# A chunked recurrence on TensorE: small products grouped by kind over six heads, and a state held in two buffers

## What is computed

```python
def second_block(x, ...):
    h = rmsnorm(x, pre_mix_g[l])
    ya, yb, yc = jnp.split(h @ w_in[l], [A_COLS, A_COLS + B_COLS], axis=-1)
    mix = jnp.concatenate([rwkv7_mixer(ya, ...), moba_mixer(*jnp.split(yb, 3, axis=-1)),
                           gmlp_mixer(...)], axis=-1) @ w_out[l]
    ...

def rwkv7_mixer(...):
    ...
    def step(state, inp):                       # once per token, 512 tokens
        r_t, w_t, k_t, v_t, kk_t, a_t = inp
        sa = jnp.einsum('bhij,bhj->bhi', state, -kk_t)
        state = (state * w_t[:, :, None, :]
                 + sa[..., :, None] * (kk_t * a_t)[:, :, None, :]
                 + v_t[..., :, None] * k_t[:, :, None, :])
        return state, jnp.einsum('bhij,bhj->bhi', state, r_t)
    _, y = lax.scan(step, s0, xs)
```

## Time and profile before

| | |
|---|---|
| median of three runs | 3281.07 us (3279.92 to 3281.27) |
| the profiled execution, first to last instruction (span) | 3270.9 us |
| its granted TensorE clock, mean | 0.987 |
| TensorE (PE) busy | 3179.8 us, 97% of the span |
| TensorE's weight loads (PEld) busy | 1976.4 us, 60% |
| VectorE (DVE) busy | 1372.5 us, 42% |
| ScalarE (ACT) busy | 598.2 us, 18% |

### The profile page before, as it was taken

How to read it: one execution, slowest core, us unless ns; L and a number is a source line. 1 busy time by engine, 2 the same in 40 slices (tenths; PEclk the granted TensorE clock), 3 DMA queues, 4 the chain that set the end, 5 groups by cost and what they waited for, 6 DMA issues and landing times.

```text
span 3270.9 us, 35828 instructions
## 1 busy us (share of the span) xinstructions
PE 3179.8 (97%) x14634; PEld 1976.4 (60%) x14634; DVE 1372.5 (42%) x2564; ACT 598.2 (18%) x1240; POOL 1.4 (0%) x6
## 2 busy tenths in 40 slices
PE   8999999999999999999999999999999999999998
PEld 5855554334333433458786588888546444688887
DVE  4256530111111111165743364466353894364655
ACT  2143220110010001121442320102332002120001
POOL 0000000000000000000000000000000000000000
PEclk9999999999999999999997999999999999999999
DMA  6122369999999999931000222222111222222221
GB/s 268 60 78 93 114 250 411 428 428 429 429 428 429 429 428 429 428 138 37 26 1 1 93 87 78 86 95 103 55 52 52 77 77 77 77 78 103 78 78 52
DMA packets 43100, 585.39 MB, mean 179 GB/s; under 512 B 4768, under 2 KB 6816, under 8 KB 7648
## 3 DMA queue, kind: packets, MB, share of 16 engines
q1 hardware_dynamic: 42752, 582.45, 43.8%
q0 software_dynamic: 224, 1.18, 0.1%
HBM read 581.51 MB, written 2.10 MB: 178 GB/s over the span
## 4 chain that ended last, share of the span: by engine, by line
PE 87%; DMA 9%; DVE 3%; ACT 1%; issue 1%; SPq 0%; DVEq 0%; ACTq 0%
PE PS L482 20%; PE PS L294 11%; PE PS L1670 11%; PE PS L686 10%; DMA ring<-in_weights 5%; PE PS L1648 4%; DMA A<-in_weights 4%; PE PS L1246 3%; PE PS L374 2%; PE PS L1593 2%; PE PS L348 2%; PE PS L1634 1%; PE PS L1575 1%; PE PS L2198 1%; PE PS L1038 1%; PE PS L1203 1%
## 5 line engine op out<-in xcount | busy, mean ns | idle before, releaser
L482 PE MATMUL PS<-A 128*128 128x256 f32 x1336 | 298.4, 380 | 0.0
L1670 PE MATMUL PS<-ring,A 128*64 128x512 f32 x1248 | 284.8, 599 | 1.5 <-DMA ring<-in_weights 0.6
L482 PEld LDWEIGHTS PS<-A 128*128 128x128 f32 x1336 | 254.1, 190 | 35.1 <-issue 0.8
L294 PE MATMUL PS<-H,ring 128*128 128x512 f32 x544 | 234.4, 593 | 0.7 <-issue 0.7
L1752 DVE TENSOR_TENSOR A<-A,PS 64x512 f32<-64x512 f32 x64 | 44.1, 690 | 434.6 <-ACT A L1699 434.6
L482 PE MATMUL PS<-H,ring 128*128 128x256 f32 x784 | 185.3, 380 | 0.8 <-ACT A L1785 0.8
L1670 PEld LDWEIGHTS PS<-ring,A 128*64 128x64 f32 x1248 | 82.7, 136 | 168.0 <-issue 160.8
L294 PEld LDWEIGHTS PS<-H,ring 128*128 128x128 f32 x544 | 103.5, 190 | 130.0 <-issue 130.0
L1670 PE MATMUL PS<-A 128*64 128x512 f32 x784 | 178.4, 598 | 2.0 <-DMA A<-in_weights 0.8
L686 PE MATMUL PS<-A 128*128 128x256 f32 x800 | 178.7, 379 | 0.0
L1648 PE MATMUL PS<-A 128*64 128x512 f32 x768 | 174.3, 598 | 3.4 <-DMA A<-in_weights 3.1
(11 more groups left out here) (534 smaller groups left out, 4126.9 us busy)
## 6 DMA issues: line engine op xcount, KB each, us to landing
ring<-in_weights SPq DMA_DIRECT2D x176, 2048.0 KB, 14.2
A<-in_weights SPq DMA_DIRECT2D x96, 2048.0 KB, 24.3
X<-in_x SPq DMA_DIRECT2D x1, 2048.0 KB, 12.9
H<-in_weights SPq DMA_DIRECT2D x1, 2048.0 KB, 13.6
A<-in_weights SPq DMA_DIRECT2D x2, 768.0 KB, 23.8
vec<-in_vec SPq DMA_DIRECT2D x1, 1047.0 KB, 11.1
A<-in_ctx SPq DMA_DIRECT2D x1, 1024.0 KB, 19.1
out_y<-X SPq DMA_DIRECT2D x2, 512.0 KB, 2.9
```

Of the source, the lines that this page charges most:

```text
L294: mm = nc.tensor.matmul(bank[:, 0:out_width], weight_tile(name, n), moving(k), start=k == 0, stop=k == k_tiles - 1)
L482: mm = nc.tensor.matmul(pair_bank(name, p, n), w[:, k, :], x[:, k, :], start=k == 0 and not more, stop=k == 3, skip_group_check=more)
L1670: mm = nc.tensor.matmul(PS[CAP * up:CAP * (up + 1), c % 2, :], XS[:, k, CAP * b:CAP * (b + 1)], expert_tile(slot, 8 * (k % 4) + 4 * up), s ...
```

## The change

It touches the loop over the chunks, on TensorE and on VectorE, and one definition:

- **Order within a group.** W, Delta and Y are issued kind by kind: one kind of product for all six heads, then the next kind for all six. W begins with the part within the chunk (128 rows), and the state's part (64 rows) comes second. Y begins with `TOK2[0] x SC2[3]`, then the state's part, then `WU[1] x SC2[1]`. The number of products and their shapes stay.
- **Flags.** Since groups of several heads are now open in one bank at once, only the first product into a bank (and into each half of its partitions) carries `start=True`; all others add, or write where nothing was written since.
- **Delta before the wait.** Its half that does not depend on U (`TOK2[2] x TOK2[0]`) is issued before TensorE waits for `u_out`.
- **State in two buffers.** `STATES[0]` and `STATES[1]` lie side by side; chunk `c` reads `STATES[c % 2]`, and the update writes the other. VectorE no longer waits for Y of this chunk (`y_chunk`, c + 1) before the update but for Y of the chunk before (`y_chunk`, c), and for none in chunk 0.

```diff
--- before.py
+++ after.py
@@ -2484,7 +2484,7 @@
         TOK2 = (tok384(A[:, 49:52, :]), tok384(H[:, 0:3, :]), tok384(H[:, 3:6, :]))
         YI = (H[:, 6, :], H[:, 7, :], a(52))
         WU = (a(46)[:, 0:384], a(47)[:, 0:384])
-        STATE = a(48)[:, 0:192].rearrange("p (a i) -> p a i", a=3)
+        STATES = [a(48)[:, 192 * n:192 * n + 192].rearrange("p (a i) -> p a i", a=3) for n in range(2)]
         LM = small[:, 384:396].rearrange("p (a c) -> p a c", a=3)
         LE = small[:, 396:408].rearrange("p (a c) -> p a c", a=3)
         SCL = small[:, 408:420].rearrange("p (a c) -> p a c", a=3)
@@ -2610,13 +2610,15 @@
             for c in range(4):
                 if c:
                     pe.wait_ge(S["state"], c)
+                STATE = STATES[c % 2]
                 for h in range(6):
-                    rows, p, i = half64(h), h // 2, slice(64 * h, 64 * h + 64)
-
-                    o = PS[:, h % 2, p * 64:p * 64 + 64]
-                    if c:
-                        nc.tensor.matmul(o, KR[p][rows, c, 0, :], STATE[rows, p, :], start=True, stop=False)
-                    mm = nc.tensor.matmul(o, SC2[h][:, c, 2, :], TOK2[0][:, c, i], start=c == 0, stop=True)
+                    mm = nc.tensor.matmul(PS[:, h % 2, h // 2 * 64:h // 2 * 64 + 64], SC2[h][:, c, 2, :],
+                                          TOK2[0][:, c, 64 * h:64 * h + 64], start=h < 2, stop=True, skip_group_check=True)
+                if c:
+                    for h in range(6):
+                        rows, p = half64(h), h // 2
+                        mm = nc.tensor.matmul(PS[:, h % 2, p * 64:p * 64 + 64], KR[p][rows, c, 0, :], STATE[rows, p, :],
+                                              start=False, stop=True, skip_group_check=True)
                 mm.then_inc(S["w"], 1)
                 moba_steps(pe, 6 * c)
                 pe.wait_ge(S["w_out"], c + 1)
@@ -2625,23 +2627,34 @@
                     mm = nc.tensor.matmul(PS[:, 0, i], SC2[h][:, c, 0, :], WU[0][:, i], start=True, stop=True)
                 mm.then_inc(S["u"], 1)
                 moba_steps(pe, 6 * c + 2)
-                pe.wait_ge(S["u_out"], c + 1)
                 if c < 3:
+                    delta = lambda h: PS[half64(h), 1, h // 2 * 64:h // 2 * 64 + 64]
                     for h in range(6):
-                        rows, p, i = half64(h), h // 2, slice(64 * h, 64 * h + 64)
-                        o = PS[rows, 1, p * 64:p * 64 + 64]
-                        nc.tensor.matmul(o, TOK2[1][:, c, i], WU[1][:, i], start=True, stop=False)
-                        mm = nc.tensor.matmul(o, TOK2[2][:, c, i], TOK2[0][:, c, i], start=False, stop=True)
+                        i = slice(64 * h, 64 * h + 64)
+                        nc.tensor.matmul(delta(h), TOK2[2][:, c, i], TOK2[0][:, c, i], start=h < 2, stop=True,
+                                         skip_group_check=True)
+                    pe.wait_ge(S["u_out"], c + 1)
+                    for h in range(6):
+                        i = slice(64 * h, 64 * h + 64)
+                        mm = nc.tensor.matmul(delta(h), TOK2[1][:, c, i], WU[1][:, i], start=False, stop=True,
+                                              skip_group_check=True)
                     mm.then_inc(S["delta"], 1)
+                else:
+                    pe.wait_ge(S["u_out"], c + 1)
                 if c:
                     pe.wait_ge(S["y_kept"], c)
+                y_chunk = lambda h: PS[half64(h), 2, h // 2 * P:(h // 2 + 1) * P]
                 for h in range(6):
-                    rows, p, i = half64(h), h // 2, slice(64 * h, 64 * h + 64)
-                    o = PS[rows, 2, p * P:(p + 1) * P]
-                    if c:
-                        nc.tensor.matmul(o, STATE[rows, p, :], KR[p][rows, c, 1, :], start=True, stop=False)
-                    nc.tensor.matmul(o, WU[1][:, i], SC2[h][:, c, 1, :], start=c == 0, stop=False)
-                    mm = nc.tensor.matmul(o, TOK2[0][:, c, i], SC2[h][:, c, 3, :], start=False, stop=True)
+                    nc.tensor.matmul(y_chunk(h), TOK2[0][:, c, 64 * h:64 * h + 64], SC2[h][:, c, 3, :], start=h < 2,
+                                     stop=True, skip_group_check=True)
+                if c:
+                    for h in range(6):
+                        rows, p = half64(h), h // 2
+                        nc.tensor.matmul(y_chunk(h), STATE[rows, p, :], KR[p][rows, c, 1, :], start=False, stop=True,
+                                         skip_group_check=True)
+                for h in range(6):
+                    mm = nc.tensor.matmul(y_chunk(h), WU[1][:, 64 * h:64 * h + 64], SC2[h][:, c, 1, :], start=False,
+                                          stop=True, skip_group_check=True)
                 mm.then_inc(S["y_chunk"], 1)
                 moba_steps(pe, 6 * c + 4)
             moba_output(pe, HEADS2 - 1)
@@ -2894,10 +2907,11 @@
                 if c < 3:
                     dve.wait_ge(S["delta"], c + 1)
                     d = PS[:, 1, 0:192].rearrange("p (a i) -> p a i", a=3)
-                    dve.wait_ge(S["y_chunk"], c + 1)
                     dve.wait_ge(S["decays"], 4)
+                    STATE = STATES[(c + 1) % 2]
                     if c:
-                        link(dve, "dve", nc.vector.tensor_tensor(STATE, STATE, d, ALU.add))
+                        dve.wait_ge(S["y_chunk"], c)
+                        link(dve, "dve", nc.vector.tensor_tensor(STATE, STATES[c % 2], d, ALU.add))
                     else:
                         link(dve, "dve", nc.vector.tensor_copy(STATE, d))
                     nc.vector.tensor_tensor(STATE, STATE, SCL[:, :, c:c + 1].to_broadcast([P, 3, 64]), ALU.mult
```

## The result

The changed kernel took 3247.31 us (median of four runs, 3245.86 to 3253.68), the kernel before 3280.49 us (3279.57 to 3281.27). The ratio is 0.9902, with a 95% interval of 0.9890 to 0.9914: 33.2 us less. Forecast were 26 us less, and 3249 us as the lowest value of the range. The direction, the mechanism and the likeliest case held; the size was too small by 7 us.

The account below looks back on a forecast made before the run. TensorE's own work was taken to bound the kernel. Savings of 16.0 us (W, Y) and 13.0 (clock), less 1.0 for waits, made 28.0, taken as 26 off 3281.1: 3255 us, own case 3252 to 3259, full range 3249 to 3269.

Parts of the forecast that it names:

- the base of the sum: Whole run: the median was taken as the profiled span of 3270.9 us plus 10.2 us around it, 3281.1.
- 28.0 forecast: Stage: W and Y save 16.0 us, the clock 13.0, new waits cost 1.0, if no clock fall stays.
- the allowance: Stage clock: a fall that stays gives back 3.1 to 6.1 us; none or one expected, so 26 us taken.
- new waits: TensorE behind shorter U and Y groups: new waits, with some overlooked, cost 1.0 us.
- The change of form: W and Y, chunks 1 to 3: each change between product shapes costs 0.15 us.
- the second of two products into one place: W and Y rival: gaps belong to adding to another's result, not to form; about 3277 us, chance 0.04.
- Row halves: 64-row runs of W and Y: neighbours in different row halves overlap, six taking 0.64 us.
- loads of two row halves queue: W and Y rival: 64-row runs take 1.28 us, 3.8 us less saved; 3259 us, chance 0.15.
- The clock: Behind W, chunks 1 to 3: three half-clock stretches of 30.7 us no longer occur, saving 13.0 us.
- the return to the half clock: Stage rival: the clock falls as before, tied to idleness rather than W's gaps; 3266 us, chance 0.20.
- Rival 4: Stage: small idle pieces in every step keep the clock at half to the stage's end; 3299 us, chance 0.03.
- State, Delta, flags: Stage: second state buffer with earlier update, Delta's half ahead of its wait, and flags each gain 0.

Follow-up runs that it names:

- x1: The kernel before the change, run again with no edit: 3281.2 us.
- x5: The changed kernel, run again with no edit: 3247.69 us.
- x12: The changed kernel with three extra 0.86 us products just behind the stage, 2.6 us of added work: 3254.4 us.
- x7: The changed kernel with W's and Y's kinds reordered to need fewer changes of form: 3249.2 us.
- x6: The changed kernel with the 64-row products of W and Y taking heads 0, 2, 4, then 1, 3, 5: 3254.1 us.
- x2: The kernel before with only W issued kind by kind; Delta, Y and state as before: 3259.4 us.
- x3: The kernel before with only Y issued kind by kind; W, Delta and state as before: 3267.4 us.
- x8: The changed kernel with W taking the kinds for two heads at a time: 3253.1 us.
- x4: The kernel before with only two state buffers, the earlier Y count and Delta's half ahead of the wait: 3280.86 us, ratio 1.0000.
- x9: The changed kernel with W and Y by kinds kept, but Delta, state buffer and waits as before: 3252.4 us.
- x11: The changed kernel with two extra 0.86 us products just behind the stage, 1.7 us of added work: 3247.7 us.
- x10: The changed kernel with one extra 0.86 us product just behind the stage: 3251.4 us.

## Why the prediction was right in its mechanism and short in its size

**The step that failed is the base of the sum.** The prediction's words were that "the median of the runs is the span and 10.2 us around it". What lies around a span is 1.8 us (x1). The other 8.4 us were the difference between the profiled execution and the usual one, which has a longer fall in the stage, one more ahead of it and three more behind it. With 1.8 in place of 10.2 the prediction's own 26 us give 3270.9 - 26 + 1.8 = 3246.7 us, and its 3252 to 3259 become 3244 to 3251: the measured 3247.3 lies in them. So the expected gain was that of a kernel which ran better than the timed one does. Like against like the sum stands: 28.0 forecast, 28.9 measured in the stage. Against a usual execution, x1, the stage went from 105.2 to 75.3, 29.9 us, and the span from 3279.5 to 3246.1 (x5), 33.4. Behind the stage x1 took 1470.9 us and x5 1466.6, 4.3 less (and ahead of it x5 was 0.8 later). There x1 has 13.8 us at half clock, and x5 has the one fall that this window holds, 0.23 / 0.5 of 7.30 us or 3.4:

```profile
1845.00:1852.30 7.30, 4.67 (x15) 3.51 (x14) 5.77 (x16) 6.25 (x13) 0.00 (x0) 0.77 0.27 61
...
2440.00:2470.00 30.00, 26.32 (x87) 13.49 (x86) 11.94 (x30) 8.71 (x24) 0.00 (x0) 1.00 0.19 70
...
2835.00:2850.00 15.00, 12.38 (x58) 10.61 (x57) 9.06 (x25) 12.33 (x27) 0.00 (x0) 1.00 0.38 141
```

A microsecond at half clock costs 0.45 us by the forecast's ratio of 1.82, so 10.4 us of it are 4.7: the size fits. No step of the prediction gives these 4.3 us. They lie in code that the change does not touch, other kernels with the same stage lose them again (x12 took 3254.4 us), and so they are luck and no gain of the new order.

**The second cut was the allowance.** "One that stays gives back 3.1 us" took 2 us off the 28; none stayed. And the "1.0" for new waits did not come: TensorE's waits are those of before (2.9 us, 3.0 before), and its idle time in the stage's windows is 1.1 us in both kernels. Without these two the forecast from the wrong base would have been 3252.

**The change of form: right.** 0.15 us each was read from W and from Y; W came out at 2.30 for 2.22, Y at 2.37 for 2.37, and x7 took away nine changes for 1.0 us, 0.12 each. x7 also shows that the second of two products into one place pays nothing.

**Row halves: right.** One pair of rows was taken over the bound. Measured, six take 0.82 us with a change. The Trainium skill (TensorE: Matmul & The Clock Gate, Part 2) has a load's time go by its columns alone and gives row tiling no path of its own; that loads of two row halves queue was the prediction's own step from there. In the trace the runs of W take 0.11 a product, against 0.16 with neighbours in one half (x6) and 0.213 for a product alone, so the loads of two row halves do not queue.

**The clock: right, and its weakest step is now shown.** "If it no longer falls" was an inference from three cases. x2 (no fall, Y untouched) and x3 (all falls, W untouched) show that the order within W decides about these three falls, and x8 that it does so by degrees. The forecast's 13.0 us for it can be set beside x2: its stage is 19.9 us shorter than x1's, of which 5.9 were given to W itself, which leaves 14.0 for the clock. Since x1 has 3.4 us more at half clock there than the execution of the forecast, 13.0 + 0.45 x 3.4 = 14.5 would be the forecast for it. The Trainium skill (same page, Part 1) ties the return to the half clock to an idle TensorE. For the three falls behind W the trace does not agree. Ahead of the first of them TensorE was busy throughout at the full clock, in the profile of before (first line) and in x1 (second line), and the changed kernel kept the full clock with TensorE idle 1.1 of 56.9 us:

```profile
1719.70:1729.96 10.26, 10.26 (x54) 6.26 (x50) 4.32 (x13) 3.90 (x11) 0.00 (x0) 1.00 0.00 0
1721.60:1728.30 6.70, 6.70 (x29) 3.49 (x29) 3.36 (x10) 2.77 (x7) 0.00 (x0) 1.00 0.00 0
```

The busy time of a row counts a record to its modelled end, so the gaps of a change of form do not show in it as idle; what the rows rule out is a wait. The prediction had argued this from 10.24 of 10.24 us behind the fall, which says nothing of what stood before it. Other falls do stand at an idle TensorE: the 17 us at the stage's start come right behind an idle stretch of 1.95 us in both kernels, and the fall of x1 at 2482.7 us stands at these two waits:

```profile
2481.24 0.55 PE L2210 MATMUL PS<-con,A 128*128 128x128 f32 x3 [1.37 <-DVE A L2253]
2482.74 1.12 PE L2210 MATMUL PS<-con,A 128*128 128x128 f32 x4 [0.95 <-DVE A L2253]
```

**Rival 4** did not come: no profile has the half clock throughout the stage, and the attention's chain added no wait of TensorE's. **State, Delta, flags**: 0 forecast, 0 in x4 (0.9991 to 1.0009) and 0.2 us in x9.

**The parts add up**: by the medians 21.6 (x2) and 13.7 (x3) make 35.3, against 33.4 for both (3281.1 to 3247.7); by the ratios 21.0 and 10.8 make 31.8, against 33.5 (x5, 0.9898); by the stages 19.9 and 7.9 make 27.8, against 29.9. The differences are within what the falls of the clock move.

## What to carry to other kernels

Small products that use different parts of TensorE's array cost little each, but every change between two such forms cost 0.15 us here, where a product takes 0.11 to 0.21: issue them kind by kind, with neighbours in different halves, and in an order whose ends match what stands around them. Here such a stretch cost more by the half clock that followed it (14.0 us in x2) than by its own length (5.9 us); look at the granted clock by windows. And before a sum is set against a median, ask whether the profiled execution is like the timed ones: here it was 8 us better, and kernels with the same stage lay up to 6.7 us apart.

## What was not expected of the hardware

Far behind the change, in code that no edit touched, the clock fell in one kernel and not in the next: 1.7 us of added work cost nothing, 2.6 us cost 6.7 (x11, x12), and 0.9 us cost 3.7 (x10). This bounds what the time of this kernel can tell of small edits, such as x7's 1.0 us, which only the stage's length shows.

Two row halves ran beside each other even where the program did not put them next to one another: with three products of one half ahead of three of the other, the six took 1.09 us and not 1.43 (x6).
